# Decoder trunk on one core: GEMMs by halves of the tokens in tile order, sums and normalisation by halves, six weight slots, TensorE's program unrolled

## The reference

```python
def rmsnorm(x, g):
    y = x * lax.rsqrt(jnp.mean(x * x, axis=-1, keepdims=True) + RMS_EPS)
    return y * g
# layer 0: in-projection (z 2048 | xBC 3072 | dt 32), causal conv, chunked SSD scan over 32 heads,
#          SiLU gate, grouped RMS norm, out-projection 2048 -> 1024
# both layers: squared_relu_mlp(x, w_up, w_down): h = relu(x @ w_up); (h * h) @ w_down, 1024 -> 4096 -> 1024
# layer 1: shared k|v projection of h, query projection of norm_pre(h), partial rotary,
#          differential attention over 8 heads (the samples over 256 cached positions), o-projection
```

## Time and profile before

| | |
|---|---|
| three timed runs | 1716.46, 1725.03, 1726.29 us; median 1725.03 us |
| the profiled execution | 1717.08 us, its span 1715.3 us |
| TensorE's granted clock, mean | 0.948 of 2.4 GHz |
| data | 142.07 MB read, 16.16 MB written, 92 GB/s over the span |

### The profile page before, as it was taken

The page is one execution under the profiler, slowest core; times in us unless marked ns, Lnnn a source line. Parts: engine busy times, 40 slices in busy tenths (PEclk is TensorE's granted clock), DMA queues, the critical chain, the costliest instruction groups (busy, mean ns, idle before and its releaser), DMA issues.

```text
span 1715.3 us, 29078 instructions
## 1 busy us (share of the span) xinstructions
PE 1556.7 (91%) x11978; PEld 1464.6 (85%) x11978; DVE 1005.1 (59%) x1387; ACT 654.9 (38%) x1301; POOL 151.8 (9%) x108
## 2 busy tenths in 40 slices
PE   7999688997997999999996999866687999999995
PEld 7999466997897999999995999733377999999995
DVE  6677889799526443244437257987845643234434
ACT  5434322899424431133225222344544432123321
POOL 0001678000000000000000000043400000000000
PEclk9999899998998999999997999978888999999998
DMA  4222000564221222222221243613111222222221
GB/s 157 77 87 87 27 7 13 188 231 172 74 94 54 93 92 90 95 89 96 87 98 62 75 136 126 202 55 124 50 38 62 87 86 99 86 99 86 97 87 62
DMA packets 44164, 159.61 MB, mean 93 GB/s; under 512 B 5026, under 2 KB 5410, under 8 KB 43810
## 3 DMA queue, kind: packets, MB, share of 16 engines
q1 hardware_dynamic: 44066, 158.25, 27.2%
HBM read 142.07 MB, written 16.16 MB: 92 GB/s over the span
## 4 chain that ended last, share of the span: by engine, by line
PE 73%; DVE 19%; ACT 3%; issue 3%; DMA 2%; POOL 1%; SPq 0%; DVEq 0%; ACTq 0%
PE GP L440 22%; PE GP L442 22%; PE GP L441 22%; DVE hT L1365 1%; DVE fT L1357 1%; DVE misc L1512 1%; DVE wL L1141 1%; DVE hs L1311 1%; PE WP L710 1%; PE WP L697 1%; DVE hc L1314 1%; DVE yss L1315 1%; PE WP L769 1%; DVE aL L1353 1%; DMA hs<-ssm_in 1%
## 5 line engine op out<-in xcount | busy, mean ns | idle before, releaser
L440 PE MATMUL GP<-aH,wH 128*128 128x260 f32 x1920 | 555.9, 290 | 32.8 <-DVE aL L1353 21.0
L442 PE MATMUL GP<-aH,wL 128*128 128x260 f32 x1920 | 550.6, 287 | 0.0
L441 PE MATMUL GP<-aL,wH 128*128 128x260 f32 x1920 | 549.0, 286 | 0.0
L440 PE MATMUL GP<-hidH,wH 128*128 128x260 f32 x1536 | 439.3, 286 | 4.1 <-DVE hidL L1325 4.1
L442 PE MATMUL GP<-hidH,wL 128*128 128x260 f32 x1536 | 434.5, 283 | 0.0
L441 PE MATMUL GP<-hidL,wH 128*128 128x260 f32 x1536 | 433.4, 282 | 0.0
L440 PEld LDWEIGHTS GP<-aH,wH 128*128 128x128 f32 x1920 | 369.5, 192 | 40.0 <-issue 30.1
L441 PEld LDWEIGHTS GP<-aL,wH 128*128 128x128 f32 x1920 | 370.1, 193 | 0.1
L442 PEld LDWEIGHTS GP<-aH,wL 128*128 128x128 f32 x1920 | 369.7, 193 | 0.0
L1141 DVE TENSOR_TENSOR wL<-wraw,wH 128x1024 fp32r<-128x1024 f32 x216 | 265.8, 1234 | 105.0 <-ACT wH L841 101.3
L440 PEld LDWEIGHTS GP<-hidH,wH 128*128 128x128 f32 x1536 | 289.9, 189 | 7.0 <-DVE hidL L1325 3.5
(11 more groups left out here) (252 smaller groups left out, 1759.3 us busy)
## 6 DMA issues: line engine op xcount, KB each, us to landing
wraw<-wblk SPq DMA_DIRECT2D x216, 512.0 KB, 3.3
hs<-ssm_in SPq DMA_DIRECT2D x16, 512.0 KB, 3.6
sssm<-hs SPq DMA_DIRECT2D x16, 512.0 KB, 3.0
ktile<-kcache SPq DMA_DIRECT2D x16, 512.0 KB, 3.6
vtile<-vcache SPq DMA_DIRECT2D x16, 512.0 KB, 4.3
hT<-x_t SPq DMA_DIRECT2D x4, 520.0 KB, 5.7
kt_out<-kT SPq DMA_DIRECT2D x1, 2080.0 KB, 10.6
vt_out<-vT SPq DMA_DIRECT2D x1, 2080.0 KB, 9.7
```

Source lines behind the costliest of these rows:

```text
L440: pe.matmul(out, lh, rh, start=first, stop=False)
L441: pe.matmul(out, lh, rl, start=False, stop=False)
L442: return pe.matmul(out, ll, rh, start=False, stop=last)
```

## The change

- ORDER and PLACE list each GEMM as halves (m, h): here m outside, h inside, throughout (EDGES is empty). half does all k of one tile for one half of the tokens, and only then come the other 260 tokens of the tile. `done` counts halves, as does `taken`.
- Six weight slots (WIDE) for blocks from out's fifth to q's last and from o's fifth on, four elsewhere; the two added ones lie in the region of yT. SLOT, TURN and FREE are worked out ahead. A slot is free when the second half of its tile is done. reach(q) is the last block whose slot was freed two halves before q or earlier; the calls of ahead now go by it.
- PSUM: single banks in place of pairs, six of them for the MLPs and the first four tiles of q, four elsewhere. The next norm's sum moves to the banks W[0] and W[1], after tile 10 (6 for q) in place of 4.
- TensorE's and SyncE's programs have no loops.
- The boundary by halves: half 0 of all tiles is summed (post_sum(p, 0), at k=4 or 6 of the last half), normalised and split while TensorE does the last half; the last half is copied and squared at m=6 of half 0 (MARKS), with a call of ahead before it; post_sum(p, 1) is at k=6 of the next GEMM's first half; before half 1 and at its m=3 ahead is called again. The last tile's squares are not added by VectorE but by a second matmul. Eight stores of y become 8 of two tiles by half.
- The operands of k are made inside q, one half tile after each of q's; the lambdas come behind the last of them.
- Squares, relu, rsq: four buffers of 260 columns in place of two of 520.

```diff
-RING = 4
+RING, WIDE = 4, 6
...
+EDGES = {}
+ORDER, PLACE = {}, {}
+for _n, _mt, _ in GEMMS:
+    _h, _t = EDGES.get(_n, (0, 0))
+    ORDER[_n] = ([(m, h) for h in range(2) for m in range(_h)] + [(m, h) for m in range(_h, _mt - _t) for h in range(2)]
+                 + [(m, h) for h in range(2) for m in range(_mt - _t, _mt)])
+    for _i, (_m, _hh) in enumerate(ORDER[_n]):
...
+def wide_block(b):
+    return BLOCK0["out"] + RING <= b < BLOCK0["k"] or b >= BLOCK0["o"] + RING
...
+SLOT, TURN, FREE = [], [], []
+_users = [[] for _ in range(WIDE)]
+for _b_ in range(NBLK):
+    _s = min(range(WIDE if wide_block(_b_) else RING), key=lambda i: (_users[i][-1] if _users[i] else i - WIDE))
+    SLOT.append(_s)
+    TURN.append(len(_users[_s]) + 1)
+    FREE.append(FREED[_users[_s][-1]] if _users[_s] else -1)
+    if _b_ >= BLOCK0["o"] + RING:
+        FREE[-1] = max(FREE[-1], PLACE["o", 0, 0])
+    _users[_s].append(_b_)
...
+def reach(q):
+    b = 0
+    while b + 1 < NBLK and FREE[b + 1] <= q - 2:
+        b += 1
+    return b
...
+        def half(name, m, h, inH, inL, each_k=None):
+            q, nk = PLACE[name, m, h], BLOCKS[name]
+            if BANK_BEFORE[q] is not None:
+                pe.wait_ge(taken, BANK_BEFORE[q] + 1)
             for kb in range(nk):
...
+                b = BLOCK0[name] + m * nk + kb
                 for k in range(8):
+                    kk = kb * 8 + k
                     if each_k is not None:
...
+        def post_sum(p, h):
+            pe.wait_ge(accf, 14 * p + ADDS[EDGE_OF[p]][6, h] + 1)
+            pe.matmul(W[h][:, 0:HALF], cc(C_ONE), acc[:, HV[h]], start=True, stop=False)
+            pe.wait_ge(sqf, 16 * p + PLACE[EDGE_OF[p], 7, h] - 2 * TILE0[EDGE_OF[p]] + 1)
+            pe.matmul(W[h][:, 0:HALF], cc(C_ONE), sqt[:, square_slot(p, 7, h), :], start=False, stop=True).then_inc(ps_mm, 1)
+        def boundary_hooks(p, name, first):
...
+        def first_gemm(name, p):
+            at = (0, 6)
+            def at_half(m, h):
+                def hook(k):
+                    if h == 0 and (m, k) == at:
+                        post_sum(p, 1)
+                    if m == 0:
+                        low_k(p)(k, h)
+                return hook
+            half_way = 6 if name == "q" else 10
+            gemm(name, aH, aL, at_half=at_half, tiles=(0, half_way))
+            pe.wait_ge(acch, 14 * (p + 1))
             for h in range(2):
...
+                if p < 3 and h:
+                    ahead(reach(PLACE[nxt, 0, 0]))
                 for m in range(KT):
...
+                    if p < 3:
+                        sc.wait_ge(h_n, 16 * p + 8 * h + m + 1)
+                        A(aH[:, m, HV[h]], hT[:, m, HV[h]], ACT.Copy, scale=pc(gpre, m)).then_inc(ahi, 1)
+                        A(fT[:, m, HV[h]], hT[:, m, HV[h]], ACT.Square).then_inc(sqh, 1)
+                        if h and m == 3:
+                            ahead(reach(PLACE[nxt, 1, 0]))
+                    if h == 0 and m in MARKS[p]:
+                        square(last + 1 + MARKS[p].index(m))
 
         def pre_norm(p):
...
+        def take_down(p, i):
+            nm = EDGE_OF[p]
+            m, h = ORDER[nm][i]
+            q = 2 * TILE0[nm] + i
+            ahead(reach(q))
+            v.wait_ge(done, q + 1)
+            if i == 0:
+                v.wait_ge(taken, q)
+            TT(fT[:, m, HV[h]], fT[:, m, HV[h]], bank(q), ALU.add).then_inc(taken, 1)
+            v.wait_ge(taken, q + 1)
+            TT(fT[:, m, HV[h]], fT[:, m, HV[h]], r2[:, HV[h]], ALU.mult).then_inc(f_s, 1)
+            v.wait_ge(f_s, 16 * (p // 2) + i + 1)
+            if i and ORDER[nm][i - 1][0] < 7:
...
+            def edge(i):
+                if p % 2:
+                    take_down(p, i)
+                else:
+                    ahead(reach(2 * TILE0[nm] + i))
+                    if ORDER[nm][i][0] < 7:
+                        add_sq(p, i)
+            for i in range(last + 1):
+                edge(i)
+            for h in range(2):
+                t, n0 = HV[h], 16 * p + 8 * h
+                def lows(m):
+                    v.wait_ge(ahi, KT + n0 + m + 1)
+                    STT(aL[:, m, t], hT[:, m, t], pc(gpre, m), aH[:, m, t].bitcast(F32), ALU.mult, ALU.subtract
+                        ).then_inc(alo, 1)
+                def scaled(m):
+                    TT(fT[:, m, t], fT[:, m, t], rpost[:, t], ALU.mult).then_inc(fr_s, 1)
+                if p < 3 and h:
+                    ahead(reach(PLACE[nxt, 0, 0]))
+                v.wait_ge(rp_s, 2 * p + h + 1)
+                scaled(0)
                 for m in range(KT):
...
+                    if m + 1 < KT:
+                        scaled(m + 1)
+                    v.wait_ge(fr_s, n0 + m + 1)
+                    STT(hT[:, m, t], fT[:, m, t], pc(gpost, m), hT[:, m, t], ALU.mult, ALU.add).then_inc(h_n, 1)
+                    if m and p < 3:
+                        lows(m - 1)
...
+        for i in range(16):
+            ahead(reach(2 * TILE0["q"] + i))
+            if i < 7:
+                pre_sum(1, 2 * i)
+                pre_sum(1, 2 * i + 1)
+            c, e = i % 8, HV[i // 8]
+            v.wait_ge(qhi, i + 1)
+            STT(hL[:, c, e], hT[:, c, e], pc("kv", c), hH[:, c, e].bitcast(F32), ALU.mult, ALU.subtract).then_inc(qlo, 1)
...
```

More of the change, by code:

```diff
@@ new lines, in half, with gemm @@
+                        each_k(kk)
+                    lh, ll = wH[SLOT[b]][:, k * P:(k + 1) * P], wL[SLOT[b]][:, k * P:(k + 1) * P]
+                    ins = three(bank(q), lh, ll, inH[:, kk, HV[h]], inL[:, kk, HV[h]],
+                                kb == 0 and k == 0, kb == nk - 1 and k == 7)
+            ins.then_inc(done, 1)
+        def gemm(name, inH, inL, after=None, each_k=None, tiles=None, inside=None, at_half=None):
+            a, e = tiles or (0, TILES[name])
+            for m, h in ORDER[name][2 * a:2 * e]:
+                if at_half is not None:
+                    hook = at_half(m, h)
+                elif m == 0:
+                    hook = each_k and (lambda k, h=h: each_k(k, h))
+                else:
+                    hook = inside and h == 0 and (lambda k, m=m: inside(m, k)) or None
+                half(name, m, h, inH, inL, hook)
+                if h == 1 and after is not None:
+                    after(m)
@@ L848, in rsqrt, with rsqrt_half @@
                   bias=misc[:, 8:9]))
+            A(dst, dst, ACT.Exp, scale=-0.5).then_inc(signal, 1)
+        def rsqrt_half(dst, sums, n, signal):
+            own(A(dst, sums, ACT.Ln, scale=1.0 / n, bias=misc[:, 8:9]))
             A(dst, dst, ACT.Exp, scale=-0.5).then_inc(signal, 1)
@@ L1032, in mlp @@
-                hidden_hi(32 * l + 16 * v + 15, 15)
+                for i, (m, h) in enumerate(ORDER[name]):
+                    n = 64 * l + 32 * v + i
+                    q = 2 * TILE0[name] + i
+                    ahead(reach(q))
+                    if v == 0 and i == 20:
+                        pre_norm(2 * l)
+                    sc.wait_ge(done, q + 1)
+                    if i == 0 and v:
+                        sc.wait_ge(taken, q)
+                    if n >= 4:
+                        sc.wait_ge(u_sq, n - 3)
+                    A(rel[:, n % 4, :], bank(q), ACT.Relu).then_inc(taken, 1)
+                    if i:
+                        hidden_hi(n - 1, ORDER[name][i - 1])
@@ L1209, in _ @@
         for m in range(NCONV):
-            ahead(m + 2)
+            ahead(reach(PLACE["xbc", m, 0]))
             if m == 5:
@@ L1428, in mlp @@
-            add_sq(KT - 1, sqf, accf, 8 * p)
-        boundary(0, "ssd_post", "mlp_pre0", True)
-        mlp(0)
-        boundary(1, "mlp_post0", "attn_pre", False)
-        pre_sum(1)
-        ahead(BLOCK0["k"] - 1)
+                    for i, (m, h) in enumerate(ORDER[name]):
+                        q = 2 * TILE0[name] + i
+                        ahead(reach(q))
+                        v.wait_ge(done, q + 1)
+                        if i == 0:
+                            v.wait_ge(taken, q)
+                        v.tensor_copy(fT[:, m, HV[h]], bank(q)).then_inc(taken, 1)
```

474 lines of the change are left out of this document (223 added, 251 removed).

## The result

The changed kernel takes 1741.74 us (median of 4 runs, 1741.49 to 1741.93), the kernel before 1720.74 us beside it (4 runs, 1715.18 to 1726.29): a ratio of 1.0125, 95% interval 1.0097 to 1.0152. It is slower by 1.25%, as forecast (1745 us, range 1713 to 1760); the interval is clear of no change, but its lower end (0.97%) is just under the 1% that the prediction took as its bound. The profiled execution has a span of 1739.4 us against 1715.3, 24.1 us more; the prediction's sum was 25.1.

What follows compares the result with a forecast made beforehand. TensorE, busy 91% of the span, was taken as the bound. The terms summed to +25.1 us on the profiled 1717.08, giving 1742.2; with +3 the forecast was 1745 us, own range 1732 to 1757, with the first rival 1713 to 1760.

Steps and rivals of the forecast that it cites:

- the clock terms: Lower clock level in and after trickling starts: 1.5 us in xbc, 2.0 in out, 2.0 at each of three boundaries.
- the end: Behind the last matmuls of down1b, the last normalisation by halves and the store: 2.9 us less.
- Steady flow, unrolling, slots and banks at nothing: Steady blocks stay at 5.74 us; loop turns removed, six weight slots and six banks gain nothing there.
- Order of the tokens in a start: The second token half follows the whole trickle of low parts: +4.8 us in out, +2.7 in xbc, 0 in o.
- Operations of half width: VectorE at 260 columns: tensor_tensor 0.425 us, scalar_tensor_tensor about 0.48, starting 0.35 and 0.40 apart; +0.6 us in v.
- Steps 1 to 4 of a boundary: VectorE starts at T0+3.5, stops twice for weights, 4.0 us each, tile 1 at T0+32.35; boundaries +4.6, +5.3, -1.9 us.
- the first rival: At the boundaries the stops for weights cost nothing, so not slower: 1718 us; chance 0.17.
- step 4: Half 1 of a boundary: 9.4 us on VectorE and another 4.0 for two weight conversions at m=3, together 13.65.
- Lambda: Between q and k, the lambda products come behind the last half's operands, so TensorE waits: +2.4 us.
- The second rival: After each of five starts the lower clock stays through a whole further block: 1759 us; chance 0.18.
- z at nothing: From z to the first block of out, the prediction put a change of 0 us.
- The +3 for the median: 3 us added to the profiled execution's footing, because the same kernel's runs sit at 1717 or at 1725.

Runs made afterwards that it cites:

- b1_unrolled: The kernel before with TensorE's loops over tiles written out, nothing else changed: 1715.75 us, ratio 0.9999.
- e5_fourslots: The changed kernel with four weight slots in place of six: 1742.98 us, ratio 1.0139.
- e2_korder: The changed kernel with the first tile of xbc and of out in the old order, k outside and token halves inside: 1728.73 us, ratio 1.0072.
- e9_storefirst: The changed kernel with SyncE's store of a state tile in z ahead of the weight load: 1733.85 us, ratio 1.0082.
- e10_edges_store: e8_edges with SyncE's store in z ahead of the weight load, as in e9_storefirst: 1670.4 us, ratio 0.9706.
- e3_zorder: The changed kernel with ScalarE's order in z as before, one block ahead fewer and both silus after the whole tile: 1738.09 us, ratio 1.0098.
- e8_edges: The changed kernel with stops, first tiles and lambda products mended, several tiles by halves at normalisations, two conversions ahead of half 1: 1676.97 us, ratio 0.9751.

## Why the prediction was right, and where it wasn't

The direction and the steps of the boundaries were right by their mechanism. That the sum came within 1 us of the measured 24.1 is luck: the clock terms were some 5.5 us too high and the end 1.5, while z's 7.0 us and xbc's 1.8 had no term at all.

- **Steady flow, unrolling, slots and banks at nothing**: right. Blocks at 5.74 us in both traces, b1_unrolled at 0.9999, e5_fourslots not to be told from the changed kernel. By the Trainium skill ("Runtime: NRT & Kernel Launch", Instruction fetch mechanics) a taken branch stalls where its target lies outside the fetched pages, and writing the loops out would then give time back. The equal blocks and b1_unrolled show no such stall here.
- **Order of the tokens in a start**: right in its mechanism, and shown by undoing it. out +4.9 against 4.8 without the clock, xbc +3.9 against 2.7 and 1.5 for the clock.
- **Operations of half width**: 0.42 for a tensor_tensor and 0.48 for a scalar_tensor_tensor, starting 0.34 and 0.40 us after each other, as worked out.
- **Steps 1 to 4 of a boundary**: right within 1.1 us for T0 to tile 1 in all three. Taking the stops away gave, within 1.2 us, the times of the first rival, so its condition (the stops cost nothing) was the wrong part, not its sum. One sum in step 4 is off: 9.4 and 4.0 make 13.4, not 13.65; the trace has 13.3 (552.94 to 566.21).
- **Lambda**: +2.1 against 2.4, and gone when the products are made earlier.
- **The end**: -4.4 against -2.9. From T0 (here 1717.2, the last matmul of tile 7's first half) VectorE starts at +4.3 (4.2), has taken the last half tile at +10.7 (11.2) and starts half 1 at +13.4 (14.1); that is 0.6 us of the difference. The other 0.9 is a matter of counting: the first sum's four matmuls stand in the second half, so the last matmul comes at T0+6.6 and not at T0+5.74, and what is counted behind it is shorter by as much.

```profile
1721.52 0.77 DVE L1503 TENSOR_TENSOR fT<-fT,rpost 128x260 f32<-128x260 f32 x2 [2.63 <-ACT rpost L940]
...
1727.49 0.43 DVE L1474 TENSOR_TENSOR fT<-fT,r 128x260 f32<-128x260 f32 x1
...
1730.66 0.77 DVE L1503 TENSOR_TENSOR fT<-fT,rpost 128x260 f32<-128x260 f32 x2 [2.21 <-ACT rpost L940]
...
1735.79 0.88 DVE L1513 SCALAR_TENSOR_TENSOR hT<-fT,pv,hT 128x260 f32<-128x260 f32 x2
```

- **The clock, 2.0 us at each of three boundaries and 2.0 in out**: too large. Behind the trickles it cost 0.1, 1.3 and 1.2 us at the boundaries and 0.1 in out; xbc's 1.5 was near (3.9 less 2.7). The order of the work alone does not fix it: from out to up0a tile 1 starts at T0+31.7 in the changed kernel and in e2_korder, and its block has 0.11 us over 5.74 in the one and 1.05 in the other. In the seven traces with one half tile on the old side it is 0.1 to 1.5 us a boundary. The second rival (a whole further block at the lower level, 4.7 us each) came nowhere.
- **z at nothing**: the step that was missing. I priced the edits in z as engine time and didn't look at what a shift of its start does to three 512 KB transfers a tile on one queue. It cost 7.0 us, and hid most of the error in the clock terms. That the order on SyncE's queue carries it is shown by e9_storefirst and e10_edges_store. What ends the long pattern early in some kernels and late in others stays open. It isn't the time of z's start alone: e2_korder enters z at 310.8 us, e3_zorder at 310.7 and e5_fourslots at 310.9, and only the first has most of the short pattern. Both traces with TensorE's order of before have it short, six of the seven with the new order and SyncE's old one have it long.
- **The +3 for the median**: the medians of before and after lie 3.7 and 0.3 us above the profiled executions' own times (1717.08 and 1741.49). So the forecast of 1745 is 3.3 us too high, nearly all of it this term. The upper end of the own range, 1757, doesn't follow from the terms: 28 us on 1717.08, with the 3, make 1748.

## What to carry to other kernels

When work is cut in halves so that one half hides behind the other engine's matmuls, first ask what each in-order engine does between the halves: here two stops for weight conversions at each of three boundaries cost 17 us together, and e8_edges had its conversions where VectorE waits anyway. Then give the hidden half enough cover: with one half tile a boundary cost 14 to 18 us, with two to four on the old side and four on the new 4 to 10. Where load, store and next load of a buffer share a queue, try the transfer that others wait for first: here it turned stores of 6 us into stores of 3.

## What the runs showed that I had not expected

- Three 512 KB transfers issued within 1 us land in 6.2 us for the store, against 2.9 to 3.0 when it goes out apart from the loads, and in the changed kernel the bad order lasted for eight stores of sixteen.
- In some kernels the granted clock dips behind xbc's 68 small matmuls on dts (at 90.3 to 92.7 us in the changed kernel) and in others it doesn't, with the same code there: 7 us of the changed kernel, always busy, hold 48 matmuls, 7 us of before 61. The block there has 1.6 us over 5.74 in the changed kernel, 0.11 in e5_fourslots and e9_storefirst, but 1.6 again in e10_edges_store. What decides stays open.

```profile
93.00:100.00 7.00, 7.00 (x48) 7.00 (x47) 3.91 (x9) 1.33 (x2) 0.00 (x0) 0.76 0.03 9
```

```profile
89.00:96.00 7.00, 7.00 (x61) 7.00 (x60) 4.67 (x11) 1.41 (x5) 0.00 (x0) 1.00 0.08 18
```

- The stretch of attention takes from 156.0 to 162.5 us over 5.74 between kernels whose code there is the same. It may be part of the spread of some 10 us that most of these kernels have from run to run; no run separates it.
